# A third Strassen step in the w_ff2 groups of a two-block transformer kernel

## The chip, the cores and the metric

The kernel runs on one core of one Trainium2 chip. Its engines are TensorE (PE, matmuls; PEld is its weight load), VectorE (DVE), ScalarE (ACT), GpSimd (POOL, unused here) and SyncE (SP, which issues the loads). The metric is the device time of one execution in microseconds; lower is better.

## The reference

Two transformer blocks are applied to x, 256 tokens by 2048 features, in float32. The first block ends in a feed-forward part, and only this part is touched:

```python
h = rmsnorm(x, g_mlp[l])
u = jnp.square(jax.nn.relu(jnp.einsum('bsd,df->bsf', h, w_ff1[l])))   # 256 x 8192
x = x + jnp.einsum('bsf,fd->bsd', u, w_ff2[l])                        # w_ff2 is 8192 x 2048
```

The second block ends in `(silu(gate) * val) @ w_down`, with w_down of 5632 x 2048.

## The kernel before, in words

Every float32 operand is split into a high part, which TensorE's fp32r format holds, and the remainder, the low part. A product is high x high + high x low + low x high: three matmuls. Weights arrive as *units* of 512 KB, 128 partitions of 1024 values (two chunks of 128 rows by 512 columns), into five RAW buffers. `split_to` (L338) does the split of each: ScalarE copies RAW into WH (the high part), then VectorE subtracts, RAW minus WH into WL (the low part). WH and WL have five buffers each (`NS = 5`), and `AHEAD = 4`: when TensorE has been given entry e, the split of e + 4 is put into the queues of ScalarE and VectorE, and that split must wait until TensorE has done with entry e - 1, whose buffer it takes. What follows (post-processing of the stage before, kept in Python generators) is put into the same two queues by `pump()`, once or twice after each entry. So each engine's order is fixed when the program is built.

w_ff2 is worked on in four segments of 2048 rows (16 chunks). In each segment, four items over w_ff1 make u for 2048 features; then *groups* multiply by w_ff2. A group covers 1024 output columns and 8 pairs of chunks (`pairs` L196, `group_item` L507). Segments 0 to 2 have two groups each (g = 0 and g = 1) and segment 3 has one, seven in all. The last 1024 columns of segment 3 go through plain items.

A plain pair is a 256-row by 256-deep by 1024-column product: 2 chunks x 2 token blocks x 2 column halves x 3 = 24 matmuls of 512 columns, from 2 entries. A Strassen pair (in the code, a "seven") splits it into 2 x 2 blocks and needs 7 products instead of 8, 21 matmuls. It has 4 entries: `left` (both chunks of the left columns, 6 matmuls), `b22` (3), `t13` (6) and `t24` (6). The last two are sums of weight blocks, which VectorE makes: `sums13` (L316) into T13, which is the memory of PB, queued just before the split of `left`; `sums24` (L328) into T24, the memory of PT, queued just after it, in two instructions. In the profile these are `PB<-RAW`, `PT<-RAW,PB` and `PT<-RAW,PT`. Where the two RAW buffers of the pair are not side by side in order, `sums13` takes two instructions of half the size. Each entry is then split like a unit.

The left operand needs sums too. `sums_x` (L596) takes four sums of blocks of u from TA into AS, four small VectorE instructions, and splits them into AXH (ScalarE) and AXL (VectorE). `sevens_x` (L1150) calls it, in the post-processing of the w_ff1 item that holds the pair: pairs 4 and 5 both belong to item g = 2. The five PSUM results of the Strassen pairs in a group gather in four banks of their own and are added into XT by `sevens_evac` (L575) after the last Strassen pair of the group, one ScalarE copy and six VectorE instructions. They must be done before the next group or item takes these banks.

Which pairs are Strassen pairs is a table, L20:

```python
SEVEN = {"ff": (2, 4), "down8": (4, 5), "down6": (3,)}
```

"ff" holds for the seven w_ff2 groups. "down8" holds for the four w_down groups of 8 pairs, and there pairs 4 and 5 are neighbours. "down6" holds for the two short w_down groups.

Of the kernel before, what the change touches and what calls it, by code (L numbers as in the profile page):

```python
# [4 lines left out]
P = 128  # L5
# [11 lines left out]
WARM = 8  # L17
ER_STEP = 16
UNIT = 1024
SEVEN = {"ff": (2, 4), "down8": (4, 5), "down6": (3,)}  # L20


C_ID, C_J, C_TRI, C_ONE, C_M, C_IC = 0, 128, 256, 384, 512, 768
# [53 lines left out]
def build(nc, io):  # L77
    f32, f32r = mybir.dt.float32, mybir.dt.float32r
    ALU, AF, AX = mybir.AluOpType, mybir.ActivationFunctionType, mybir.AxisListType.X
    add, sub, mul, mx = ALU.add, ALU.subtract, ALU.mult, ALU.max  # L80

    ctx = ExitStack()
    with ctx:
        def sb(name, shape, dt=f32, c=ctx):
            return c.enter_context(nc.sbuf_tensor(name, shape, dt))

        def sem(name):
            return ctx.enter_context(nc.semaphore(name))
# [16 lines left out]
        SQ = sb("SQ", [P, 512])  # L105
# [19 lines left out]
        MHL = sb("MHL", [P, NKC, 2 * T], f32r)  # L125

        with ExitStack() as c:
            AXH = sb("AXH", [P, 2, 4, P], f32r, c=c)
            AXL = sb("AXL", [P, 2, 4, P], f32r, c=c)
            AS = sb("AS", [P, 4, P], c=c)  # L130
            EV = sb("EV", [P, 2, 512], c=c)
            sb("QK2pad", [P, 4096 - 1536 - 2048], c=c)
            GF = sb("GF", [P, D], c=c)
        with ExitStack() as c:
            Q2 = sb("Q2", [P, 8, T], c=c)
# [3 lines left out]
        AHL = sb("AHL", [P, 8, 2 * T], f32r)  # L139
        CHL = sb("CHL", [P, 8, 2 * T], f32r)  # L140
        PS = ctx.enter_context(nc.psum_tensor("PS", [P, 8, 512], f32))
        T13 = PB[:].rearrange("p a b -> p (a b)")[:, 0:1024]
        T24 = PT[:].rearrange("p a b -> p (a b)")[:, 0:1024]
        ERD = nc.dram_tensor("er_scratch", [P, 8, 384], f32).ap()
# [18 lines left out]
        V = Queue(sem("s_dve"))  # L163
        A = Queue(sem("s_act"))
        SP = Queue(None)
        mm, tt, ts = nc.tensor.matmul, nc.vector.tensor_tensor, nc.vector.tensor_scalar
        stt = nc.vector.scalar_tensor_tensor
        act = nc.scalar.activation
# [27 lines left out]
        def pairs(w, row0, kcs, col0, name):  # L196
# [3 lines left out]
            if key not in made:  # L200
                made[key] = steps = []
                for n in range(len(kcs) // 2):
                    first = len(units)
                    for half in range(2):
                        r, c = row0 + 2 * n * P, col0 + 512 * half
                        units.append((w[r:r + 2 * P, c:c + 512].rearrange("(k p) n -> p k n", p=P), 2, 512))
                    seven = n in SEVEN[name]
                    steps.append((seven, len(ents), kcs[2 * n:2 * n + 2]))
# [86 lines left out]
        def paired(e):  # L295

            return WH[:, e % NS, 0:NKC * 16].rearrange("p (k n) -> p k n", k=NKC)

        def landed(u):
            return (s_raw[u % NR], 16 * (u // NR + 1))  # L300
# [15 lines left out]
        def sums13(u):  # L316
# [3 lines left out]
            if b > a:  # L320
                return V.step(tt, T13.rearrange("p (h n) -> p h n", h=2), RAW[:, b, :].rearrange("p (h n) -> p h n", h=2),
                              RAW[:, a:a + 2, 0:512], sub, after=[landed(u), landed(u + 1), t_free[0]])
            for i in range(2):
                v = V.step(tt, T13[:, 512 * i:512 * i + 512], RAW[:, b, 512 * i:512 * i + 512], left[i], sub,
                           after=[landed(u), landed(u + 1), t_free[0]])
            return v

        def sums24(u):  # L328

            a, b = u % NR, (u + 1) % NR  # L330
            V.step(tt, T24[:, 0:512], RAW[:, b, 512:1024], T13[:, 0:512], sub)
            t_made[u] = V.step(tt, T24[:, 512:1024], RAW[:, a, 512:1024], T24[:, 0:512], sub)
# [5 lines left out]
        def split_to(e):  # L338
            while state["split"] <= min(e, len(ents) - 1):
# [8 lines left out]
                if what in ("t13", "t24"):  # L348
                    raw, at, done = (T13, T24)[what == "t24"], [t_made[u]], None
                if what == "b22":  # L350
# [64 lines left out]
        def feature_item(parts, src, tok, mid=(), small=False, ahead=AHEAD):  # L415
# [3 lines left out]
            for n, (u, kcs, banks, first, last) in enumerate(parts):  # L419
# [4 lines left out]
                for k, kc in enumerate(kcs):  # L424
# [3 lines left out]
                    for j0 in range(0, len(banks), 2):  # L428
                        two = list(enumerate(banks))[j0:j0 + 2]
                        for j, bank in two:  # L430
                            PE.do(mm, PS[:, b + bank, :], h[:, k, j * P:(j + 1) * P], src[:, kc, :],
                                  start=st, stop=False, inc=False)
                        for j, bank in two:
                            end = j == len(banks) - 1 and k == len(kcs) - 1
                            t = PE.do(mm, PS[:, b + bank, 0:T], l[:, k, j * P:(j + 1) * P], src[:, kc, 0:T],
                                      start=False, stop=en, inc=end)
# [11 lines left out]
        def f_item():  # L448
# [6 lines left out]
            for kc in kcs:  # L455
                t = PE.do(mm, PS[0:16, b, :], paired(u)[:, kc, :], XHL[:, kc, :], start=kc == 0, stop=kc == NKC - 1,
                          inc=kc == NKC - 1)
# [3 lines left out]
            def rest():  # L461
                tk["ft"] = V.step(nc.vector.tensor_reduce, FTR[:], PS[0:16, b, :].rearrange("p (h t) -> p t h", h=2),
                                  AX, add, after=[t])
                free[s] = [tk["ft"]]
                yield
# [6 lines left out]
        def token_item(units_, src, tok, n, mid=(), at=None, hold=False, tail=False):  # L472
# [4 lines left out]
            for i, (u, kcs) in enumerate(units_):  # L477
# [7 lines left out]
                for k, tb in order:  # L485
# [3 lines left out]
                    xl = src[:, kc, T + tb * P:T + (tb + 1) * P]  # L489
                    o = PS[:, b + tb, 0:n]  # L490
                    PE.do(mm, o, xh, h[:, k, :], start=i == 0 and k == 0, stop=False, inc=False)
# [15 lines left out]
        def group_item(steps, src, tok, stok, mid=(), tail=False):  # L507
# [6 lines left out]
            for n, (seven, e, kcs) in enumerate(steps):  # L514
# [21 lines left out]
                else:  # L536
# [6 lines left out]
                    a22 = src[:, kcs[1], P:T], src[:, kcs[1], T + P:2 * T]  # L543
                    s1, s2, s3, s4 = ((AXH[:, i, j, :], AXL[:, i, j, :]) for j in range(4))
                    for work in (((bp, a11, 0, o, c), (b, a12, 1, False, False)),
# [21 lines left out]
        def three(bank, xh, xl, h, l, first, last, inc):  # L567
            PE.do(mm, PS[:, bank, :], xh, h, start=first, stop=False, inc=False)
            PE.do(mm, PS[:, bank, :], xh, l, start=False, stop=False, inc=False)
            return PE.do(mm, PS[:, bank, :], xl, h, start=False, stop=last, inc=inc)  # L570

        ax_free = {}
# [23 lines left out]
        def sums_x(seven, j, tok, after):  # L596


            a11, a21, a12, a22 = (TA[:, j + i, tb * P:(tb + 1) * P] for i in range(2) for tb in range(2))
            V.step(tt, AS[:, 0, :], a21, a22, add, after=after)  # L600
            V.step(tt, AS[:, 1, :], AS[:, 0, :], a11, sub)
            V.step(tt, AS[:, 2, :], a11, a21, sub)
            v = V.step(tt, AS[:, 3, :], a12, AS[:, 1, :], sub)
            a = A.step(act, AXH[:, seven], AS[:], AF.Copy, after=[v, ax_free.get(seven)])
            tok[seven] = V.step(tt, AXL[:, seven], AS[:], AXH[:, seven].bitcast(f32), sub, after=[a])

        def group(w, row0, kcs, g, name):
            steps = pairs(w, row0, kcs, 1024 * g, name)
# [314 lines left out]
        def rel_item():  # L923
# [18 lines left out]
               add, after=[(s_id, 16)])  # L942
# [207 lines left out]
        def sevens_x(half_seg, name, tok, after):  # L1150

            for i, pair in enumerate(SEVEN[name]):
                if pair // 2 == half_seg:
                    sums_x(i, 2 * (pair % 2), tok, after)
                    yield
# [45 lines left out]
        for seg in range(4):  # L1201
            utok, stok = {}, {}
            for g in range(4):
                if seg == 1 and g == 0:

                    SP.dma(nc.sync.dma_start, BIAS[:], bass.AP(ERD.tensor, ERD.offset + P - 1, [[8 * 384 - 1, P], [384, 8], [1, T]]),
                           s_wp, after=[er_t, branches_t])
# [315 lines left out]
```

How the kernel before makes its waits and increments, by code:

```python
    def play(self, eng):  # L67
        for step in self.prog:
            if step[0] == "wait":
                eng.wait_ge(step[1], step[2])
            else:
                ins = step[1](*step[2], **step[3])
                if step[4]:
                    ins.then_inc(*step[4])
```

## Time and profile before

| | |
|---|---|
| median of 3 runs | 2388.35 us (2388.16 to 2389.65) |
| the profiled execution, its own time | 2390.3 us |
| its span (first to last instruction) | 2388.2 us |
| PE busy | 2378.5 us, 100% of the span |
| PEld busy | 2035.8 us, 85% |
| DVE busy | 1700.8 us, 71% |
| ACT busy | 1216.2 us, 51% |
| granted TensorE clock, mean | 0.999 |
| data moved | 452.14 MB, mean 189 GB/s |

All operations are recorded through one helper, so every row has line L72; rows are told apart by the names of the tiles, output first: `WL<-PB,WH` is the low part of a t13 entry. A busy PE is not PE at its peak, since matmuls overlap in these records; the distance between the starts of two matmuls tells its pace.

### The profile page before, as it was taken

To read this page: it belongs to the slowest core of one execution; us is meant where nothing else is said; L and a number is where in the kernel's file an instruction comes from. 1 tells how busy PE (TensorE), PEld (TensorE's weight loads), DVE (VectorE), ACT (ScalarE), POOL (GpSimd) and SP (SyncE) were. 2 spreads that over 40 slices of the span, in tenths; PEclk is the share of its full clock that TensorE was granted. 3 is DMA by queue.
4 is the path that set the end of the run, shared out by engine and by line. 5 is a ranking of instruction groups with operands and counts; after the bars stand their busy time and mean duration, and the time that the engine had idled before them with its cause. 6 is when DMAs were issued, how large, how long until landed. Compare 5 with 4: busy or idle time off the path is not lost.

```text
span 2388.2 us, 30674 instructions
## 1 busy us (share of the span) xinstructions
PE 2378.5 (100%) x12581; PEld 2035.8 (85%) x12581; DVE 1700.8 (71%) x1804; ACT 1216.2 (51%) x1427; POOL 0.2 (0%) x4
## 2 busy tenths in 40 slices
PE   9999999999999999999999999999999999999999
PEld 8788888888888888888888888888888888888887
DVE  5565666666567868868868667855788777886788
ACT  5354454555544545445445555555555455545554
POOL 0000000000000000000000000000000000000000
PEclk9999999999999999999999999999999999999999
DMA  7557566665565675656665565555655665566655
GB/s 252 160 162 204 161 196 192 192 188 197 189 185 172 216 223 183 218 175 203 200 192 188 183 185 168 168 177 185 186 181 193 199 193 177 183 217 189 187 171 181
DMA packets 238040, 452.14 MB, mean 189 GB/s; under 512 B 16570, under 2 KB 20780, under 8 KB 237772
## 3 DMA queue, kind: packets, MB, share of 16 engines
q1 hardware_dynamic: 237147, 449.07, 59.4%
q8 instruction: 98, 1.61, 0.3%
q10 hardware_dynamic: 752, 1.12, 0.1%
q14 instruction: 43, 0.34, 0.0%
HBM read 446.46 MB, written 3.67 MB: 188 GB/s over the span
## 4 chain that ended last, share of the span: by engine, by line
PE 96%; DVE 3%; ACT 1%; DMA 0%; issue 0%; SPq 0%; DVEq 0%; ACTq 0%
PE PS L72 96%; DVE WL L72 1%; ACT WH L72 1%; DVE PB L72 0%; DVE PT L72 0%; DVE XT L72 0%; DMA RAW<-in_w_in 0%; DVE TB L72 0%; DVE TA L72 0%; ACT TA L72 0%; ACT SQ L72 0%; DVE XHL L72 0%; ACT TB L72 0%; DVE TC L72 0%; DVE SEL L72 0%
## 5 line engine op out<-in xcount | busy, mean ns | idle before, releaser
L72 DVE TENSOR_TENSOR WL<-RAW,WH 128x1024 fp32r<-128x1024 f32 (+1 forms) x844 | 1001.8, 1204 | 517.0 <-ACT WH L72 514.9
L72 PE MATMUL PS<-XHL,WH 128*128 128x512 f32 x3984 | 1254.1, 396 | 2.2 <-DVE CR L72 1.3
L72 ACT ACTIVATE WH<-RAW 128x1024 fp32r<-128x1024 f32 (+1 forms) x845 | 867.1, 1041 | 735.7 <-PE PS L72 721.4
L72 PEld LDWEIGHTS PS<-XHL,WL 128*128 128x128 f32 x3968 | 746.1, 188 | 176.3
L72 PE MATMUL PS<-XHL,WL 128*128 128x256 f32 x3968 | 780.3, 278 | 0.0
L72 PE MATMUL PS<-WH,MHL 128*128 128x512 f32 x2000 | 624.6, 390 | 0.0
L72 PEld LDWEIGHTS PS<-XHL,WH 128*128 128x128 f32 x3984 | 607.2, 188 | 6.5 <-DVE CR L72 1.5
L72 PEld LDWEIGHTS PS<-WH,MHL 128*128 128x128 f32 x2000 | 375.5, 188 | 78.3 <-DVE XHL L72 0.4
L72 PE MATMUL PS<-WL,MHL 128*128 128x512 f32 x1000 | 389.1, 389 | 0.0
L72 PEld LDWEIGHTS PS<-WL,MHL 128*128 128x128 f32 x1000 | 187.8, 188 | 37.9
L72 ACT ACTIVATE MHL<-TA 128x1024 fp32r<-128x1024 f32 x33 | 35.0, 1061 | 121.9 <-DVE TA L72 121.9
L72 DVE TENSOR_TENSOR TA<-TA,PS 128x1024 f32<-128x1024 f32 x72 | 87.9, 1221 | 9.0 <-ACT TA L72 1.9
L72 ACT COPY TA<-PS 128x1024 f32<-128x1024 f32 x72 | 73.2, 1017 | 19.9 <-DVE PB L72 3.5
L72 PE MATMUL PS<-WH,XHL 128*128 128x512 f32 x256 | 80.6, 391 | 0.1
L72 DVE TENSOR_TENSOR XT<-XT,PS 128x1024 f32<-128x1024 f32 (+1 forms) x49 | 55.6, 1134 | 5.7 <-PE PS L72 1.1
L72 DVE TENSOR_TENSOR MHL<-TA,MHL 128x1024 fp32r<-128x1024 f32 x33 | 40.4, 1226 | 24.9 <-ACT MHL L72 23.7
L72 PEld LDWEIGHTS PS<-WH,XHL 128*128 128x128 f32 x256 | 48.1, 188 | 10.4 <-DVE TA L72 0.6
L72 ACT ACTIVATE WH<-PB 128x1024 fp32r<-128x1024 f32 x24 | 25.4, 1058 | 57.6 <-DVE PT L72 45.1
L72 DVE SCALAR_TENSOR_TENSOR TB<-TC,VEC,TB 128x256 f32<-128x256 f32 x104 | 43.2, 479 | 10.1 <-ACT TB L72 10.1
L72 PE MATMUL PS<-WL,XHL 128*128 128x512 f32 x128 | 49.9, 390 | 0.0
L72 DVE SCALAR_TENSOR_TENSOR TA<-TC,VEC,TA 128x256 f32<-128x256 f32 x88 | 36.7, 478 | 11.2 <-ACT TA L72 11.2
L72 PE MATMUL PS<-CHL,WH 128*128 128x512 f32 x128 | 40.2, 395 | 0.0
(150 smaller groups left out, 1211.2 us busy)
## 6 DMA issues: line engine op xcount, KB each, us to landing
RAW<-in_w_ff SPq DMA_DIRECT2D x256, 512.0 KB, 4.1
RAW<-in_w_in SPq DMA_DIRECT2D x224, 512.0 KB, 3.9
RAW<-in_w_up SPq DMA_DIRECT2D x176, 512.0 KB, 4.1
RAW<-in_w_down SPq DMA_DIRECT2D x88, 512.0 KB, 4.4
RAW<-in_w_mix_out SPq DMA_DIRECT2D x32, 512.0 KB, 3.9
RAW<-in_w_out SPq DMA_DIRECT2D x32, 512.0 KB, 3.7
RAW<-in_w_conv_out SPq DMA_DIRECT2D x16, 512.0 KB, 3.7
RAW<-in_w_attn_out SPq DMA_DIRECT2D x16, 512.0 KB, 4.2
```

The lines of the kernel that those rows point to most:

```text
L72: ins = step[1](*step[2], **step[3])
```

## The change

Pair 5, the sixth of a w_ff2 group, becomes a Strassen pair beside 2 and 4, in each of the seven groups. AXH and AXL get a third slot each. The room comes from a pad that goes and from AS, which moves onto SQ (the buffer for squares and for the diagonal matrices of the norms), of the same size; GF stays where it was.

```diff
-SEVEN = {"ff": (2, 4), "down8": (4, 5), "down6": (3,)}
+SEVEN = {"ff": (2, 4, 5), "down8": (4, 5), "down6": (3,)}
...
-            AXH = sb("AXH", [P, 2, 4, P], f32r, c=c)
-            AXL = sb("AXL", [P, 2, 4, P], f32r, c=c)
-            AS = sb("AS", [P, 4, P], c=c)
+            AXH = sb("AXH", [P, 3, 4, P], f32r, c=c)
+            AXL = sb("AXL", [P, 3, 4, P], f32r, c=c)
             EV = sb("EV", [P, 2, 512], c=c)
-            sb("QK2pad", [P, 4096 - 1536 - 2048], c=c)
             GF = sb("GF", [P, D], c=c)
...
+        AS = SQ[:].rearrange("p (a b) -> p a b", a=4)
...
-            a = A.step(act, AXH[:, seven], AS[:], AF.Copy, after=[v, ax_free.get(seven)])
-            tok[seven] = V.step(tt, AXL[:, seven], AS[:], AXH[:, seven].bitcast(f32), sub, after=[a])
+            a = A.step(act, AXH[:, seven], AS, AF.Copy, after=[v, ax_free.get(seven)])
+            tok[seven] = V.step(tt, AXL[:, seven], AS, AXH[:, seven].bitcast(f32), sub, after=[a])
```

## Rows read from the trace of the kernel before

**Rows 1.** The page, busy us (share of span) and instructions of each engine.
```profile
PE 2378.5 (100%) x12581; PEld 2035.8 (85%) x12581; DVE 1700.8 (71%) x1804; ACT 1216.2 (51%) x1427; POOL 0.2 (0%) x4
```

**Rows 2.** The page, the chain that ended last, by engine.
```profile
PE 96%; DVE 3%; ACT 1%; DMA 0%; issue 0%; SPq 0%; DVEq 0%; ACTq 0%
```

**Rows 3.** Busy time by windows: stretch, length, each engine's busy us, clock, DMA share, GB/s.
```profile
754.85:797.02 42.17, 42.17 (x188) 34.93 (x187) 37.24 (x36) 22.30 (x23) 0.00 (x0) 1.00 0.63 209
797.02:839.20 42.18, 42.18 (x188) 34.92 (x187) 35.32 (x34) 20.62 (x21) 0.00 (x0) 1.00 0.60 201
2058.73:2101.45 42.72, 42.47 (x189) 34.85 (x188) 37.29 (x42) 23.93 (x27) 0.00 (x0) 1.00 0.56 189
```

**Rows 4.** Groups of instructions by shape: busy us, mean ns of one, idle before.
```profile
L72 DVE TENSOR_TENSOR WL<-RAW,WH 128x1024 fp32r<-128x1024 f32 x816 | 982.7, 1222 | 513.2 <-ACT WH L72 511.1
...
L72 DVE TENSOR_TENSOR AS<-TA 128x128 f32<-128x128 f32 x26 | 7.6, 292 | 0.9
```

**Rows 5.** Timeline, DVE, first w_down group of 8 pairs: start, us, operation, idle before.
```profile
2079.00 1.23 DVE L72 TENSOR_TENSOR WL<-PB,WH 128x1024 fp32r<-128x1024 f32 x1 [0.52 <-ACT WH L72]
...
2081.49 1.23 DVE L72 TENSOR_TENSOR PB<-RAW 128x1024 f32<-128x1024 f32 x1
2082.64 1.22 DVE L72 TENSOR_TENSOR WL<-RAW,WH 128x1024 fp32r<-128x1024 f32 x1
2083.89 0.69 DVE L72 TENSOR_TENSOR PT<-RAW,PB 128x512 f32<-128x512 f32 x1
2084.61 0.69 DVE L72 TENSOR_TENSOR PT<-RAW,PT 128x512 f32<-128x512 f32 x1
2085.22 0.68 DVE L72 TENSOR_TENSOR WL<-RAW,WH 128x512 fp32r<-128x512 f32 x1
2086.43 1.23 DVE L72 TENSOR_TENSOR WL<-PB,WH 128x1024 fp32r<-128x1024 f32 x1 [0.53 <-ACT WH L72]
...
2099.93 1.22 DVE L72 TENSOR_TENSOR XT<-XT,PS 128x1024 f32<-128x1024 f32 x1
```

**Rows 6.** Timeline, PE, the same group: first matmul of either t13 entry.
```profile
2082.54 0.39 PE L72 MATMUL PS<-WH,AXH 128*128 128x512 f32 x1
...
2087.71 0.50 PE L72 MATMUL PS<-WH,AXH 128*128 128x512 f32 x1 [0.25 <-DVE WL L72]
```

**Rows 7.** Timeline, DVE, low part of pair 4's t13, three w_ff2 groups of seven.
```profile
775.36 1.23 DVE L72 TENSOR_TENSOR WL<-PB,WH 128x1024 fp32r<-128x1024 f32 x1 [0.53 <-ACT WH L72]
...
816.93 1.23 DVE L72 TENSOR_TENSOR WL<-PB,WH 128x1024 fp32r<-128x1024 f32 x1 [0.53 <-ACT WH L72]
...
1295.86 1.22 DVE L72 TENSOR_TENSOR WL<-PB,WH 128x1024 fp32r<-128x1024 f32 x1 [0.53 <-ACT WH L72]
```

**Rows 8.** Timeline, PE, first matmul of the same three t13 entries.
```profile
778.00 0.39 PE L72 MATMUL PS<-WH,AXH 128*128 128x512 f32 x1
...
820.15 0.39 PE L72 MATMUL PS<-WH,AXH 128*128 128x512 f32 x1
...
1298.47 0.39 PE L72 MATMUL PS<-WH,AXH 128*128 128x512 f32 x1
```

**Rows 9.** Timeline, DVE, the last w_ff1 item and the start of a group.
```profile
745.67 0.69 DVE L72 TENSOR_TENSOR AXL<-AS,AXH 128x512 fp32r<-128x512 f32 x1 [0.70 <-ACT AXH L72]
...
750.63 1.23 DVE L72 TENSOR_TENSOR WL<-RAW,WH 128x1024 fp32r<-128x1024 f32 x1 [0.51 <-ACT WH L72]
753.41 1.23 DVE L72 TENSOR_TENSOR WL<-RAW,WH 128x1024 fp32r<-128x1024 f32 x1 [1.56 <-ACT WH L72]
...
756.20 1.23 DVE L72 TENSOR_TENSOR WL<-RAW,WH 128x1024 fp32r<-128x1024 f32 x1 [0.20 <-ACT WH L72]
```

**Rows 10.** Timeline of PE, in the plain item behind the last w_ff2 group.
```profile
1338.27 1.09 PE L72 MATMUL PS<-CONST,XT 128*128 128x128 f32 x8 [0.66 <-DVE XHL L72]
```

**Rows 11.** Timeline of PE, before the clock falls.
```profile
89.27 0.73 PE L72 MATMUL PS<-XHL,WH 128*128 128x512 f32 x2 [1.28 <-DVE CR L72]
```

**Rows 12.** Busy time by windows, the stretch behind it.
```profile
90.00:93.40 3.40, 3.40 (x12) 2.92 (x12) 0.77 (x1) 0.66 (x2) 0.00 (x0) 0.50 0.80 243
```

## The prediction

> **What bounds the kernel now.** I read the page's engine row first [rows 1]: PE 100% busy, DVE 71%, ACT 51%. Then the chain that ended last [rows 2]: 96% of it is PE, 3% DVE. A removed matmul should therefore be worth its whole pace. But 71% is a mean over stages, and the change works in seven groups only, so the third view is the busy time by windows [rows 3]. In the first w_ff2 group (g = 0) DVE is busy 37.24 of 42.17 us, 88%; in the second (g = 1) 35.32 of 42.18, 84%. The change takes from PE and gives to DVE. The last view is the timeline of DVE and PE around a t13 entry [rows 5 to 8], which tells how early a sum of weights is ready before PE wants it.
>
> **What goes from PE.** A plain pair is 24 matmuls, a Strassen pair 21. A w_ff2 group is 6 x 24 + 2 x 21 = 186 matmuls in 42.17 us [rows 3], 0.2267 us each. Three fewer in seven groups: 21 x 0.2267 = 4.76 us. Loads are the same bytes, and PSUM evacuation has the same seven instructions, two entries later.
>
> **What comes to DVE.** Per new pair: `PB<-RAW` 1.23, two of `PT<-` at 0.69, and low parts of 1.22 + 0.68 + 1.23 + 1.22 in place of two of 1.22 [rows 4, 5]: 1.23 + 1.38 + 4.35 - 2.44 = 4.52 us. In g = 0 that makes 37.24 + 4.52 = 41.8 us of DVE work against 42.17 - 0.68 = 41.5 of PE. DVE is then full over the group, and in the pairs 4 and 5 over full: a Strassen pair lasts PE 21 x 0.2267 = 4.76 us, and DVE longer. How much longer is seen in the w_down groups, whose pairs 4 and 5 are Strassen pairs already. There the low part of t13 ends at 2079.00 + 1.23 = 2080.23 for pair 4 and at 2086.43 + 1.23 = 2087.66 for pair 5 [rows 5]: 7.43 us a pair, every DVE instruction against the next but for 0.53 us of waiting for ScalarE's copy of T13, which itself waits for `sums24`. So each neighbour costs 7.43 - 4.76 = 2.67 us of lead, and four entries of lookahead are just one such pair.
>
> **What that costs PE.** Call s the lead of pair 4's t13: start of its first matmul on PE less the end of its low part. In the w_down group s = 2082.54 - 2080.23 = 2.31 [rows 5, 6]. PE would want pair 5's t13 at 2082.54 + 4.76 = 2087.30; it gets it at 2087.71 [rows 6], 0.05 after the low part, 0.41 late, and the matmul after a stall follows somewhat later than the usual 0.23. The window has both: 42.72 us [rows 3] against 42.17, 0.55. So the cost is 0.55 + 2.31 - s = 2.86 - s, and nothing where s is larger.
>
> In the w_ff2 groups pair 4 is a Strassen pair already, so s stands in the trace. g = 0: 778.00 - 776.59 = 1.41 in segment 0 and 1298.47 - 1297.08 = 1.39 in segment 3; g = 1: 820.15 - 818.16 = 1.99 [rows 7, 8]. The seven are 1.41, 1.20, 1.39, 1.39 (g = 0) and 2.00, 2.00, 1.81 (g = 1), read alike: 11.20 together. All are shorter than w_down's because pair 2, with one plain pair between, has drawn on the lead already, and in g = 0 the post-processing of w_ff1 as well. 7 x 2.86 - 11.20 = 8.8 us.
>
> Three smaller terms. (a) In segment 3 pair 5 lies across the end of the RAW ring (unit 4 mod 5), so `sums13` is two halves: 2 x 0.69 + 0.03 against 1.23, +0.2. (b) Item g = 2 makes two sets of sums instead of one: four instructions of 0.29 with 0.03 between, then 0.70 of waiting for ScalarE and 0.69 [rows 4, 9], 2.7 us more on DVE. Of that DVE's idle time up to the group takes 0.51 + 1.56 [rows 9] and 0.25 before the first split; 0.4 to 0.5 is late at the group's `sums13`, and 0.20 of idle time stands behind that [rows 9]. I take 0.2 late in three groups and 0.4 in segment 2, where `sums13` is in halves and nothing is idle behind it: +0.9, bounds 0 and 1.9. The items themselves are not stalled, since the 16 matmuls of a w_ff1 unit hold PE for 2.8 us in the timeline and its split holds DVE for 1.2. (c) Behind g = 0 DVE is late by some two splits of 1.22. The Strassen evacuation, in w_down, ends at 2099.93 + 1.22 = 2101.15, and PE starts the next group at 2101.45 [rows 3, 5]; this 0.3 is locked to the stall, so it holds here too. In g = 1 DVE has by my count 0.8 us left when pair 4 comes, so s stays. In segment 3 a plain item follows, where PE already waits for DVE (0.66 before the second turning of XT [rows 10]) at the end of an unbroken ScalarE and DVE chain: +0.5, bounds 0 and 1.2.
>
> At nothing: the splits' DMA waits (the units of pair 5 land before DVE comes to them, as in w_down); AS on SQ (squares and diagonals lie outside the sums, on the same in-order engines); the third slot.
>
> **Sum.** +8.8 + 0.2 + 0.9 + 0.5 - 4.76 = +5.6 us. The profiled execution took 2390.3, so 2395.9 on its scale; it lies 1.95 above the median of the runs, 2388.35, which gives 2394.0.
>
> **Clock.** In this trace PE waited 1.28 us at 88 us [rows 11], behind ten small matmuls of the running sums, and the next 3.40 us ran at a granted 0.50, the lower level of 1.2 GHz [rows 12], at a loss of 1.7 us. The stall of 0.66 [rows 10] and the 0.25 in w_down [rows 6] cost no clock. The new stalls of g = 0 would be 1.3 to 1.7 us, each between dense matmuls. The Trainium skill, "TensorE: Matmul & The Clock Gate", section "A second HAM failure mode: psum-queue depth-cycling", says that frequent short idle times between groups of matmuls can make the clock swing between its levels; by this rule the change would be dearer still. The trace bears it out once, so it is a rival.
>
> **Rivals.**
> 1. *The lead holds.* DVE has its splits ready and only PE's saving is left: 2388.35 - 4.76 = 2383.6. It needs s of 2.86 or more. For it: the second w_down groups pass without a stall. Against: their lead was above 4, and none here is over 2.0. Were only pair 5's DVE time shorter, by some 1.3 us, the result would turn faster. 8%, with the time between 2383.6 and 2386.
> 2. *Half the cost.* Only g = 0 stalls, or each stall is about 0.7 shorter because DVE's order in the w_ff2 groups has less in it than in w_down: 4 x 2.86 - 5.39 = 6.1, less 4.76, +1.3; with the small terms +2.9. 2389.5 to 2391.5. 25%.
> 3. *The clock falls* after the stalls of g = 0: four times 1.7 on top, 2400.8. 6%.
> 4. *DVE's lateness is carried over*: the 0.8 us left in g = 1 is not there, each s in g = 1 is about 1 less, three times 1.0 more: 2397. 10%.
>
> My own case has 51%, 2392 to 2396.
>
> **The numbers.** 0.2%, 4.8 us, is about what a measurement of this kernel can tell from no change: 2383.6 and 2393.1 are the edges. Slower: of my case about four fifths (0.42), and rivals 3 and 4 (0.16), 0.58. Faster: the lower half of rival 1 and a margin for what I don't see, 0.07. Same: the rest, 0.35. The range goes from rival 2's lower part to short of rival 3: 2388.5 to 2398.5.
>
> **What would show it.** In the profile after, the low part of pair 5's t13 ends 7.4 us after pair 4's, and PE waits for `DVE WL` once or twice in each w_ff2 group, 1.3 to 1.7 us in g = 0 and 0.8 to 1.0 in g = 1; the g = 0 window is near 41.5 + 1.5 = 43.0 and g = 1 near 42.4. PE has 21 matmuls fewer, DVE's busy time is up by 7 x 4.5 + 4 x 1.9 = 39 us. I am wrong if no wait for WL shows, if pair 4's lead has moved by over 0.5, or if the time goes into stretches outside the groups.

## The result: 2402.7 us, slower by 0.56%

| | before | after |
|---|---|---|
| median of 4 runs each | 2389.0 us | 2402.7 us |
| ratio | | 1.0056, 95% interval 1.0044 to 1.0068 |
| span of the profiled execution | 2388.2 us | 2401.7 us |
| forecast | | 2394.0 (2388.5 to 2398.5) |

The direction was right; the size, 13.7 us, was 2.4 times the forecast's 5.6, and lies outside the range. The runs of one kernel lie at two levels about 1.5 us apart: behind PE's wait of 1.28 us near 89 us ([rows 11, 12]) the clock falls in some executions and not in others. The page after, with its lines for span, engines and chain (before: [rows 1, 2]):

```profile
span 2401.7 us, 30721 instructions
...
PE 2379.2 (99%) x12560; PEld 2030.2 (85%) x12560; DVE 1735.8 (72%) x1860; ACT 1225.7 (51%) x1445; POOL 0.2 (0%) x4
...
PE 84%; DVE 11%; ACT 3%; DMA 1%; issue 1%; DVEq 0%; SPq 0%; ACTq 0%
```

The 21 matmuls are gone (12581 to 12560). DVE's part of the chain went from 3% to 11%, and DMA stands in it with 1%, where there was 0%. That 1% is the trail. Busy time by windows, g = 0 and g = 1 of segment 0 and the first two w_down groups together (columns as in [rows 3]):

```profile
754.71:799.82 45.11, 42.58 (x185) 33.96 (x184) 39.65 (x41) 23.16 (x25) 0.00 (x0) 1.00 0.59 202
799.82:842.31 42.49, 41.91 (x185) 34.35 (x184) 39.36 (x40) 21.78 (x23) 0.00 (x0) 1.00 0.59 198
2072.20:2157.09 84.89, 84.63 (x375) 69.75 (x373) 72.67 (x77) 44.23 (x48) 0.00 (x0) 1.00 0.57 194
```

g = 1 came as forecast (42.5 against 42.4); g = 0 takes 45.1 us where 43.0 was forecast; w_down is as it was. Four times 2.1 us is 8.4, and the miss is 13.7 - 5.6 = 8.1: all of it lies in the four g = 0 groups. Who kept PE waiting there, in the timeline of PE:

```profile
767.43 0.39 PE L72 MATMUL PS<-WH,AXL 128*128 128x512 f32 x1
769.06 0.50 PE L72 MATMUL PS<-WH,AXH 128*128 128x512 f32 x1 [1.24 <-DVE WL L72]
...
784.45 0.50 PE L72 MATMUL PS<-WH,AXH 128*128 128x512 f32 x1 [0.38 <-DVE WL L72]
...
786.20 0.50 PE L72 MATMUL PS<-WH,AXH 128*128 128x512 f32 x1 [0.79 <-DVE WL L72]
```

The last two are pair 5's b22 and t13, which were expected to stall. The first, at 769.06, is pair 2's t13: a start 1.63 us behind the one before it where 0.23 is the pace. The forecast had no stall there. DVE before that group, the place of [rows 9] (AS is named SQ now):

```profile
745.54 0.69 DVE L72 TENSOR_TENSOR AXL<-SQ,AXH 128x512 fp32r<-128x512 f32 x1 [0.70 <-ACT AXH L72]
...
748.23 0.69 DVE L72 TENSOR_TENSOR AXL<-SQ,AXH 128x512 fp32r<-128x512 f32 x1 [0.70 <-ACT AXH L72]
749.19 5.77 DVE L72 TENSOR_TENSOR WL<-RAW,WH 128x1024 fp32r<-128x1024 f32 x5 [0.26 <-ACT WH L72]
757.18 1.23 DVE L72 TENSOR_TENSOR PB<-RAW 128x1024 f32<-128x1024 f32 x1 [2.23 <-DMA RAW<-in_w_ff]
```

The second set ends at 748.92, 2.7 us behind the first, as counted. DVE then does five splits in a row and catches up, as counted. But `PB<-RAW`, sums13 of pair 2, starts at 757.18 and not near 755.1, where the splits are done: DVE sits idle for 2.23 us until a load lands. The waits of DVE for loads of w_ff2, whole kernel after:

```profile
DVE PB L72 <- DMA RAW<-in_w_ff: 8.0, 4, 2.2
```

Four waits, one per segment, 8.0 us in all, the longest 2.2; before there was none. The first loads of the burst, after and then before (queue, count, first and last issue; the last line is time to landing):

```profile
L72 SPq DMA_DIRECT2D RAW<-in_w_ff x3: 367/367/368, 750.4 to 752.7; - x3
...
DMA to landing us min/median/max: 3.5/5.5/6.1
```

```profile
L72 SPq DMA_DIRECT2D RAW<-in_w_ff x4: 368/368/368, 747.9 to 751.9; - x4
...
DMA to landing us min/median/max: 3.9/5.4/5.8
```

A load is issued when the split of the unit five places earlier frees its RAW buffer. Before, the first of this burst went out at 747.9; after, at 750.4, 2.5 us later, since the splits stood behind the second set. DVE can catch up on splits; a load that went out late lands late. And these loads had nothing to spare. sums13 waits for the second of the burst: before, it went out at 749.01 and landed at 754.59, 0.18 us before sums13 began; after, it went out at 751.58 and landed at 757.10. Issued 1.1 us apart, the loads of this burst take a median of 5.4 to 5.5 us to land, where the page gives 4.1 for all loads of w_ff2.

### The profile page after: what moved, and what is told of

Same layout as the page of the kernel before. It is cut to its first block, busy times and chain, and to the rows that moved or that the text cites. A ratio compares the mean times of both kernels' runs of the same rounds, so it can differ in the third digit from the quotient of the medians.

```text
span 2401.7 us, 30721 instructions
## 1 busy us (share of the span) xinstructions
PE 2379.2 (99%) x12560; PEld 2030.2 (85%) x12560; DVE 1735.8 (72%) x1860; ACT 1225.7 (51%) x1445; POOL 0.2 (0%) x4
## 4 chain that ended last, share of the span: by engine, by line
PE 84%; DVE 11%; ACT 3%; DMA 1%; issue 1%; DVEq 0%; SPq 0%; ACTq 0%
PE PS L72 84%; DVE WL L72 6%; ACT WH L72 2%; DVE TA L72 1%; DVE PT L72 1%; DVE PB L72 1%; DMA RAW<-in_w_ff 1%; DVE MHL L72 0%; DVE SQ L72 0%; DVE XT L72 0%; ACT MHL L72 0%; DMA RAW<-in_w_in 0%; DVE TB L72 0%; ACT TA L72 0%; ACT SQ L72 0%
## 5 line engine op out<-in xcount | busy, mean ns | idle before, releaser
L72 PE MATMUL PS<-WH,MHL 128*128 128x512 f32 x1930 | 605.2, 390 | 0.8 <-DVE WL L72 0.6
L72 PEld LDWEIGHTS PS<-WH,MHL 128*128 128x128 f32 x1930 | 362.3, 188 | 77.9 <-DVE WL L72 2.5
L72 PE MATMUL PS<-WL,MHL 128*128 128x512 f32 x965 | 375.6, 389 | 0.0
L72 PEld LDWEIGHTS PS<-WL,MHL 128*128 128x128 f32 x965 | 181.2, 188 | 36.7
L72 ACT ACTIVATE WH<-PB 128x1024 fp32r<-128x1024 f32 x31 | 32.8, 1059 | 84.5 <-DVE PT L72 78.2
L72 PE MATMUL PS<-WH,AXH 128*128 128x512 f32 x124 | 50.2, 405 | 12.0 <-DVE WL L72 12.0
L72 DVE TENSOR_TENSOR MHL<-TA,MHL 128x1024 fp32r<-128x1024 f32 x33 | 40.5, 1226 | 25.3 <-ACT MHL L72 23.7
L72 DVE TENSOR_TENSOR WL<-PB,WH 128x1024 fp32r<-128x1024 f32 x31 | 37.9, 1224 | 16.1 <-ACT WH L72 16.1
```

The source lines that it names most:

```text
L72: ins = step[1](*step[2], **step[3])
```

## The experiments

Theory A: the second set holds up the splits, the splits hold the RAW buffers, the buffers hold the loads, and DVE is late by 2.5 us when the group starts. Theory B: DVE just has too much to do in g = 0 (41.8 us against 41.5). Each time is against the kernel before on the same chip. *Excess* is what the distances between the starts of PE's matmuls have over the pace of 0.227 us, added up.

**1. Pair 5 without sums of its own.** It multiplies with pair 4's, so its product is not the right one; only the timing counts here.

```diff
-                if pair // 2 == half_seg:
+                if pair // 2 == half_seg and not (name == "ff" and pair == 5):
...
-                    i = sevens.index(n)
+                    i = min(sevens.index(n), 1)
```

> The changed kernel without the second set of sums in item g = 2: pair 5 multiplies with pair 4's set (so its left operand is wrong), all else is the same. Theory A (landing): the second set holds up the splits, these hold the RAW buffers, and the loads that the group's first sums13 needs land 2.2 us late, which costs the stall at pair 2's t13 (1.5 us in each g = 0 group) and 0.5 to 0.7 us of pair 5's stall there. Without the set both go: 4 x 2.1 = 8.5 us less than the changed kernel, about +5 us against before (ratio 1.002), sums13 of the first group starts with no wait for a load, and pair 2's t13 has its lead of 0.9 us. Theory B (the rival: DVE has too much to do inside the group, whatever comes before it): the stall at pair 2 stays, ratio 1.005 or more.

Measured: 2393.4 against 2388.7, ratio 1.0019 (1.0010 to 1.0029), +4.7 us. No stall at pair 2; DVE waits for a load once, 0.3 us:

```profile
DVE PB L72 <- DMA RAW<-in_w_ff: 0.3, 1, 0.3
```

This is Theory A's number: 9.0 of the 13.7 us hang on one set of small sums, which starts 8.4 us before the group. Nothing inside the group's DVE work differs, so Theory B can't give it. This kernel also shows the formula for pair 5 undisturbed. The excess at pair 5 in the seven groups: 1.43, 1.63, 1.44, 1.63 (g = 0) and 0.84, 0.84, 1.03 (g = 1); 2.86 - s gives 1.45, 1.66, 1.47, 1.47 + 0.18 and 0.86, 0.86, 1.05.

**2. The second set alone, pair 5 plain** (`enumerate((2, 4, 5) if name == "ff" else SEVEN[name])` in `sevens_x`, "ff" back at (2, 4)).

> Pairs 2 and 4 as before, pair 5 plain, but item g = 2 makes the second set of sums all the same (nobody reads it). Theory A: sums13 waits some 2 us for its load in each of the four segments, pair 2's t13 is late by 1.4 us there, so +1.5 us in each g = 0 group, 4 x 1.5 = +6 us (ratio 1.0025), and no stall at pair 4 (lead about 0.7 left). Theory B: nothing inside the group is added, so no more than +0.5 us (ratio 1.000).

Measured: 2394.9, ratio 1.0024 (1.0015 to 1.0033), +6.3 us, with an unusual spread of 2392.2 to 2397.6. In the profiled execution, the quickest, DVE waits four times for loads, and the excess at pair 2 is 0.72, 1.29, 0.92 and 0.94. DVE's waits for loads, and PE's for DVE (two of these six are w_down's, as before):

```profile
DVE PB L72 <- DMA RAW<-in_w_ff: 6.5, 4, 2.0
...
PE PS L72 <- DVE WL L72: 3.5, 6, 1.0
```

Nothing in the group differs from before, and still it stalls: Theory B falls. The spread fits a loss that depends on when a DMA lands, but that was not shown.

**3. The second set two splits later.**

```diff
+SPACE = 3
...
                     sums_x(i, 2 * (pair % 2), tok, after)
                     yield
+                    if name == "ff" and pair == 4:
+                        for _ in range(SPACE):
+                            yield
```

> The changed kernel with the same instructions, but the second set of sums is queued two splits later than the first instead of right behind it. Theory A: the splits that free the RAW buffers of the group's third pair come between the two sets, its loads land as before, sums13 starts at most 0.5 us later than before and has no wait for a load, pair 2 has no stall, and the time is about +5.5 us against before (ratio 1.002 to 1.0025). Theory B (DVE work in sum): same work, same time, ratio 1.0055.

Measured: 2396.9, ratio 1.0032 (1.0021 to 1.0044), +8.2 us: 5.5 less than the change with the very same instructions (in the two traces, the excess in the Strassen pairs is 6.2 us less).

```profile
749.10 0.69 DVE L73 TENSOR_TENSOR AXL<-SQ,AXH 128x512 fp32r<-128x512 f32 x1 [0.70 <-ACT AXH L73]
750.05 3.50 DVE L73 TENSOR_TENSOR WL<-RAW,WH 128x1024 fp32r<-128x1024 f32 x3 [0.26 <-ACT WH L73]
753.68 1.23 DVE L73 TENSOR_TENSOR PB<-RAW 128x1024 f32<-128x1024 f32 x1
```

sums13 has no wait for a load in any segment, and pair 2's excess is nowhere more than 0.2 us. sums13 starts 0.7 us behind the group's start (752.97), and 0.7 to 1.1 in the other segments, where it was 0.1 ahead before; pair 5 in g = 0 costs 0.5 to 0.7 more than in experiment 1. So this run splits the 9.0 us: the larger part hangs on where the set stands in the queue, the rest, 3.5 us by the medians and 2.6 by the traces, on DVE being plainly late in this order. In the change itself the splits were done at 754.96, which would have put sums13 0.4 to 0.5 us later than before, relative to the group's start, as the prediction counted; no run shows what that alone would cost.

**4. Pairs 1, 3 and 5** (`SEVEN["ff"] = (1, 3, 5)`).

> Pairs 1, 3 and 5 as Strassen pairs instead of 2, 4 and 5: the same 21 matmuls fewer and the same DVE work per group, but no neighbours, and one set of sums in each of items g = 0, 1, 2. My theory of the lead (a neighbour costs 2.7 us of lead, and the second set 2.2 us): g = 1 groups have no stall and save 0.68 each; g = 0 groups may lose some at pair 1, whose sums now fall into the post-processing of w_ff1, 0 to 2 us each. -4.8 to +3 us against before, ratio 0.998 to 1.001. Rival (DVE is simply full in g = 0, 41.8 us of work against 41.5): g = 0 still costs some 2 us over its PE time at whatever pair, ratio 1.001 to 1.003.

Measured: 2401.6, ratio 1.0053 (1.0038 to 1.0068), +12.9 us. Both expectations missed it (at most 1.003). The waits of PE:

```profile
PE PS L72 <- DVE XT L72: 7.8, 6, 2.3
PE PS L72 <- DVE WL L72: 3.9, 6, 0.8
```

The new one is XT: pair 1 comes 5.4 us after a g = 1 group begins and wants the four banks that g = 0 has just left, which DVE has yet to add into XT. There are three such waits, of 2.29, 1.92 and 2.23 us, and behind the first two the clock falls. PE's first matmul after the first wait, the windows before, in and after, and the windows behind the second and the third:

```profile
798.10 0.79 PE L72 MATMUL PS<-WH,MHL 128*128 128x512 f32 x1 [2.29 <-DVE XT L72]
```

```profile
795.00:798.00 3.00, 0.81 (x4) 0.34 (x2) 2.93 (x4) 0.00 (x0) 0.00 (x0) 0.99 0.13 48
798.00:801.20 3.20, 3.10 (x7) 2.48 (x8) 3.13 (x5) 0.54 (x1) 0.00 (x0) 0.50 0.00 0
801.20:804.00 2.80, 2.80 (x13) 2.27 (x12) 2.15 (x3) 1.58 (x2) 0.00 (x0) 0.97 0.69 187
...
982.20:985.60 3.40, 3.40 (x8) 2.66 (x9) 2.15 (x2) 0.53 (x1) 0.00 (x0) 0.51 0.03 9
1160.30:1163.70 3.40, 3.40 (x15) 2.83 (x16) 2.77 (x3) 1.69 (x2) 0.00 (x0) 1.00 0.04 6
```

**5. The left operand's sums on GpSimd.** Its queue G takes the four sums and the AXL subtraction; ScalarE's copy comes one pair of pumps later.

```diff
-            V.step(tt, AS[:, 0, :], a21, a22, add, after=after)
+            G.step(gtt, AS[:, 0, :], a21, a22, add, after=[after, sq_used])
...
+            yield
+            yield
             a = A.step(act, AXH[:, seven], AS, AF.Copy, after=[v, ax_free.get(seven)])
-            tok[seven] = V.step(tt, AXL[:, seven], AS, AXH[:, seven].bitcast(f32), sub, after=[a])
+            tok[seven] = G.step(gtt, AXL[:, seven], AS, AXH[:, seven].bitcast(f32), sub, after=[a])
```

> The changed kernel with the sums of the left operand (four into AS, and the AXL subtraction) on GpSimd instead of VectorE, for all Strassen pairs of the kernel, and ScalarE's copy into AXH queued one split later, so that nothing in VectorE's queue waits for them. Theory A (the second set is dear because it holds up the splits and so the loads): nothing holds the splits now, so as with one set: about +4.5 us against before (ratio 1.002), no wait of sums13 for a load. Rival (it costs by sharing SBUF or buffers, on whatever engine): +10 us or more (1.004).

Measured: 2393.3 against 2388.5, ratio 1.0019 (1.0010 to 1.0029), +4.8 us. The full computation at the price of experiment 1: outside VectorE's queue the sums cost nothing that can be measured, so the rival (they cost on whatever engine) falls. This run takes both their work and their place from VectorE; experiment 3 is the one that tells the two apart.

**6 and 7. The weights' sums on GpSimd, alone and with the former** (`G.step` in `sums13` and `sums24`, and the RAW buffers freed by both engines).

> The changed kernel with the weights' sums (sums13, sums24, 2048 elements of 128 partitions per Strassen pair) on GpSimd; the left operand's stay on VectorE. VectorE then has 4.3 us of low parts in a Strassen pair that lasts PE 4.76 us, so a neighbour takes no lead. If GpSimd does the three sums in under 4.7 us a pair: no stall at pair 5, at most 1.5 us at pair 2 of g = 0; -4.8 to +2 us, ratio 0.998 to 1.001. Rival (GpSimd is the slower one): a stall per pair of its excess over 4.76 us in all 38 Strassen pairs' neighbours, w_down's too; ratio over 1.005.

> Both of these: all sums on GpSimd. If GpSimd keeps up, no stall is left in the groups, w_down's 0.55 and 0.77 go too: -4.8 - 1.3 - some of 0.5 = about -6 us, ratio 0.9975. If it doesn't, as the rival of the run before.

Measured: 2451.3, ratio 1.0259 (1.0242 to 1.0276), and 2450.2, ratio 1.0256 (1.0241 to 1.0272): +62.8 and +61.7 us. (The Strassen pairs are 31 in all, not the 38 of the expectation.) Groups of GpSimd by shape, in experiment 6:

```profile
L72 POOL TENSOR_TENSOR PB<-RAW 128x1024 f32<-128x1024 f32 x25 | 67.9, 2717 | 2064.2 <-DMA RAW<-in_w_ff 1004.4 <-DMA RAW<-in_w_down 780.0 <-DVE TA L72 180.0
L72 POOL TENSOR_TENSOR PT<-RAW,PB 128x512 f32<-128x512 f32 x31 | 61.0, 1968 | 2.4
L72 POOL TENSOR_TENSOR PT<-RAW,PT 128x512 f32<-128x512 f32 x31 | 54.1, 1746 | 2.4
```

2.7 + 2.0 + 1.7 = 6.4 us a pair, against PE's 4.76: the rival. In experiment 6 PE waits 42.3 us for WL in 22 places, up to 5.1 us at once, and behind the long waits the clock falls too. How the 62.8 us divide between GpSimd, VectorE's longer operations beside it and the clock was not measured.

**8. GpSimd for the left sums, and T13's copy released early.** ScalarE's copy of T13 waited for `sums24`, which only T24 needs; this is the 0.53 us of idle DVE of [rows 5].

```diff
-                    raw, at, done = (T13, T24)[what == "t24"], [t_made[u]], None
+                    raw, done = (T13, T24)[what == "t24"], None
+                    at = [(t13_made, t_made)[what == "t24"][u]]
...
-                    sums13(u)
+                    t13_made[u] = sums13(u)
```

> The changed kernel with the left operand's sums on GpSimd (as in the run before, +4.8 us) and ScalarE's copy of T13 waiting for sums13 alone, not for sums24 behind it. Theory: the 0.53 us for which DVE waits in every Strassen pair goes, so a neighbour takes 7.43 - 0.53 = 6.9 us against PE's 4.76, a lead of 2.1 instead of 2.7; and the lead at pair 4 of g = 0 grows by two such waits, 1.4 to 2.5. Cost of pair 5 then 2.3 - 2.5, nothing, in g = 0, and 2.3 - 2.5 or less in g = 1: no stall in the groups, none or little in w_down. -4.8 (matmuls) to -5.8 (w_down too), ratio 0.9975 to 0.998. Rival (DVE is full by the sum of its work, the wait is only moved elsewhere): +2 us or more.

Measured: 2384.3 against 2388.65, ratio 0.9983 (0.9974 to 0.9991), -4.4 us: faster than both kernels. Timeline of DVE, pairs 4 and 5 of the first group:

```profile
773.92 0.68 DVE L72 TENSOR_TENSOR WL<-RAW,WH 128x512 fp32r<-128x512 f32 x1
774.52 1.22 DVE L72 TENSOR_TENSOR WL<-PB,WH 128x1024 fp32r<-128x1024 f32 x1
...
780.74 0.68 DVE L72 TENSOR_TENSOR WL<-RAW,WH 128x512 fp32r<-128x512 f32 x1
781.34 1.22 DVE L72 TENSOR_TENSOR WL<-PB,WH 128x1024 fp32r<-128x1024 f32 x1
```

A pair now takes DVE 781.34 - 774.52 = 6.82 us instead of 7.43, with no idle time in front of t13. The windows of segment 0's two groups and of the first w_down groups:

```profile
754.60:837.82 83.22, 83.22 (x368) 68.63 (x367) 78.83 (x80) 46.14 (x48) 0.00 (x0) 1.00 0.63 207
2055.91:2140.24 84.33, 84.33 (x374) 69.83 (x373) 73.18 (x78) 45.28 (x48) 0.00 (x0) 1.00 0.59 197
```

83.22 is 366 x 0.2267 = 82.97 and 0.25 of stall; 84.33 is w_down without its 0.55. What keeps it from the full -6.1 is 0.2 to 0.4 a g = 0 group and the plain item behind the last Strassen group, whose wait is 1.23 us instead of 0.66.

**9. That edit on the change alone**, and **10. on the kernel before alone.**

> The changed kernel with that edit alone, the left sums all on VectorE as in the change. Theory: the second set still makes sums13 wait for its load, some 2.2 us, once per g = 0 group; pair 2's lead of 0.9 has 0.5 more to give, so its stall falls from 1.5 to about 1.0, and pair 5's goes: 4 x 1.0 + 0.5 - 4.8 = 0 us, from -2 to +2, ratio 0.999 to 1.001.

> The kernel before with that edit alone. Theory: nothing waits there but w_down's pairs 5 (0.55 and 0.77 us), which go: -1.3 us, ratio 0.9995. If it gains over 2 us, the edit does more than the theory says.

Measured: 2393.0, ratio 1.0019 (1.0010 to 1.0029), +4.3 us, where -2 to +2 was expected; and 2387.4, ratio 0.9995 (0.9986 to 1.0004), -1.2 us. The last has no clear difference in time, but in its trace w_down's two stalls (0.55 and 0.77 us) are gone, as expected. In experiment 9 DVE waits for loads four times, 7.3 us in all, and pair 2's excess is still 1.0 to 1.4. What the expectation had wrong is pair 5 in g = 0: its stall does not go, its excess is 0.9 to 1.2. I read this as the lead never being there for a group that starts so late; that was argued, not tested. So the early release and the removal of the left sums from VectorE are each worth 9 us on the change (13.7 to 4.3, 13.7 to 4.8), and only the two together get below the kernel before.

## Why the prediction was wrong

- *21 matmuls at 0.2267, -4.76 us*: right.
- *A neighbour takes 2.67 us of lead; pair 5 costs 2.86 - s*: right, and with it rivals 1 and 2 (no stall, or half of it) fall. With s undisturbed (experiment 1) every group is within 0.03 us, 8.84 in sum against 8.8 + 0.2 forecast; the 0.2 of term (a) is there in segment 3.
- *Term (c), the plain item behind segment 3, +0.5*: 1.57 to 1.59 us between two starts there instead of 1.05 before. Right. Without term (b) the forecast is 5.6 - 0.9 = +4.7 us, and experiment 1, which leaves (b) out, measured +4.7.
- *Term (b), the second set, +0.9, "bounds 0 and 1.9"*: this is the step that failed, together with the DMA waits put at nothing, the next item. It costs 9.0 us by the medians (13.7 - 4.7), 8.6 by the spans. In the trace after, the excess at pair 2 is 1.51, 1.53, 1.56 and 1.13, 5.7 us, and pair 5 in g = 0 costs 2.11, 2.32, 2.11 and 2.27, which is 2.7 us more than in experiment 1. The formula holds here too: pair 4's lead has shrunk from 1.41 to 0.68 in segment 0 (forecast 1.2), and 2.86 - 0.68 = 2.18. That is a move of over 0.5, one of the prediction's own signs of being wrong.
- *Splits' DMA waits at nothing*: I had checked the landing for pair 5's units, inside the group, and not for pair 2's, in front of which I had put a delay of my own making. I set the 2.7 us of new work against DVE's idle time and stopped; but freed buffers come late by the whole 2.5 us, whatever idle time follows, and the load that sums13 waits for needs 5.5 us after that. An upper bound worked out in this way would have been 2.5 us late in each of four segments, less the 0.9 of lead that pair 2 had, with pair 5's loss of lead on top.
- *Rival 3, the clock falls*: not here. In the trace after, PE waits up to 1.29 us in the groups, and the clock stays at its upper level behind each of these waits. The mechanism exists: in experiment 4 waits of 2.29 and 1.92 us were followed by a granted 0.50.
- *Rival 4, lateness carried into g = 1*: no; g = 1 is as forecast.
- *DVE is then full over the group (41.8 against 41.5)*: too high. In experiment 1 DVE is busy 39.6 of 42.9 us in the first g = 0 group. The count took each operation at its own duration, 1.22, but operations back to back overlap in the record: five splits take 5.77 us, not 6.1. For the same reason DVE's busy time rose by 35 us against the 39 forecast. What holds is the 7.43 us of a neighbour, which was read from start to start.

## What to carry to other kernels

Where one engine's work frees the buffers that loads go into, price its delay twice: as work, which later idle time can absorb, and as loads issued late, which nothing absorbs but the slack of their landing. So look up each load's landing against its first use around every place where something is queued. And before a product is traded for sums, read the lead by which the operands arrive in that stage; here a wait for one sum more than needed, 0.53 us a pair, and the engine that makes the small left sums made the difference between +13.7 and -4.4 us.

## What the runs showed of the hardware

- Two-input float32 operations of 128 x 1024 take a mean of 2717 ns on GpSimd (experiment 6) and 1226 on VectorE (before), and of 128 x 512 1746 to 1968 against 692; single ones of 512 took from 1262 to 2167. Small ones are far apart too: 128 x 128 took means of 715 to 1018 ns in experiment 5 against 292.
- VectorE's own operations get longer beside them. `WL<-RAW` of 128 x 512, most of which run while GpSimd makes sums, took a mean of 1525 ns in experiment 6 and 685 before:

```profile
L72 DVE TENSOR_TENSOR WL<-RAW,WH 128x512 fp32r<-128x512 f32 x35 | 53.4, 1525 | 4.9 <-ACT WH L72 4.8
```

- The time to landing of a 512 KB load grows within a burst. In the trace after, the three loads shown take 3.5, 5.5 and 6.1 us, and the two behind them 6.3 and 6.5: the page's median of 4.1 us is no bound.
- Whether the clock falls does not follow from the length of PE's wait alone. In experiment 4 it fell behind 2.29 and 1.92 us and not behind 2.23, all three between dense matmuls. The wait of 1.28 us near 89 us was followed by a granted 0.50 in the profiled executions of both kernels and of experiments 1, 6 and 8, and by 1.00 in those of the other seven.
